# Modulation vectors as products of transposed weight rows on VectorE in a fused transformer kernel (one core, float32)

## The chip, the cores and the metric

The kernel runs as one program on one core of a Trainium2 chip. The metric is device time in microseconds for one execution. The kernel before takes 2101.35 us (median of 3 runs, 2100.73 to 2102.05).

## The reference

Two blocks of two layers each work on 256 tokens of width 1024; the first layer also carries 256 context tokens, so its units see 512 columns and all later ones 256. Everything is float32. What the change touches is the modulation: each of the four layers has a matrix of 1024 x 6144 that is multiplied with one or two vectors of 1024, and the result shifts, scales and gates the activations.

```python
silu_c, silu_cc = silu(c), silu(c_ctx)
for l in range(2):                                   # first block
    sh1, sc1, g1, sh2, sc2, g2 = split(silu_c @ w_mod[l] + b_mod[l], 6)
    csh1, ..., cg2 = split(silu_cc @ w_mod[l] + b_mod[l], 6)      # context, used in l = 0 (and sh1, sc1 of l = 1)
    m = mixer(x * (1 + sc1) + sh1)                   # Fourier, neighbourhood and latent attention, gates, w_out
    x = layer_norm(ALPHA * x + (1 + g1) * m)
    f = (silu(h @ w_gate) * (h @ w_up)) @ w_down     # h = x * (1 + sc2) + sh2, hidden width 2816
    x = layer_norm(ALPHA * x + (1 + g2) * f)
for i in range(2):                                   # second block: recurrent mixer, pool mixer, squared-relu MLP
    mod = silu(c_2) @ w_mod_2[i] + b_mod_2[i]
    ...
```

## The kernel before

The program is a list of units that every engine walks in the same order. A unit computes 512 output columns of one projection in four tiles m = 0 to 3, each with 8 tiles k of 128 rows. Weights are split in two float32r parts: ScalarE writes the high part SH (L509), VectorE the rest SL (L515), and TensorE makes three products for each (m, k), L556 to L558. The split for the next unit runs while this unit's products run; SH and SL have one buffer for each m. The raw weights come in two pairs RAW0, RAW1 of 1 MB by SyncE (L503), each issued when the split of the unit before has read that pair. Banks 0 to 3 of PSUM take the four tiles.

Beside the projections the 4 x 12 modulation chunks of 512 columns are computed. Four are made in the opening; the other 44 are hosted, one for each unit. There are two ways:
- `Side` (30 chunks). SyncE loads the chunk, 2 MB with 2 KB runs, into SIDE (L359). TensorE multiplies it with the columns CC of the vectors in 8 products of 512 columns (L373, 16 records in a trace), ahead of tile m = 3 (or of the unit's first product where the unit goes by k). VectorE transposes the result in blocks (L378), TensorE gathers it into columns at the unit's end (L326), VectorE adds the bias (L395).
- `SideOnDve` (14 chunks, two in single units and the twelve of the loop of the first layer's feed-forward). VectorE multiplies and adds the 8 row tiles, 512 elements each (L417 once, L421 seven times), transposes (L426), sums (L428); TensorE gathers (L437), VectorE adds the bias (L450).

The feed-forward of the first block has five single units and a loop of two turns over six units (four `UpGated`, two `Down`), for each layer. Between layers stands a norm that needs the last unit's complete result. SyncE, ScalarE and VectorE are in-order queues: what stands behind a wait is late with it.

Of the kernel before, what the change touches and what calls it, by code (L numbers as in the profile page):

```python
# [21 lines left out]
ALU = mybir.AluOpType  # L22
ACT = mybir.ActivationFunctionType
AX = mybir.AxisListType
# [100 lines left out]
class Counts:  # L125
# [30 lines left out]
    def up(self, name, by=1):  # L156
# [9 lines left out]
           "chunk2_loaded", "chunk3_loaded", "side_loaded", "out_done"],  # L166
# [3 lines left out]
            "tap_done", "tile_squared", "out_high", "gate_copied", "gate_open"],  # L170
    "dve": ["weight_low", "dve_read", "side_summed", "side_flipped", "side_added", "dve_done", "centred", "input_low", "one_minus_a2", "scanned",
# [9 lines left out]
def build(nc, A, out, const):  # L181
# [48 lines left out]
    U = MACC[:, 4:8, :].rearrange("p a b -> p (a b)").rearrange("p (t g n) -> p t g n", t=2, g=4)  # L230

# [38 lines left out]
    EARLY1, EARLY3 = (sb(f"EARLY{j}", [P, KT, 512], at=at) for j, at in ((1, AH_AT), (3, YH_AT)))  # L270
    EARLY2 = reg("EARLY2", 2048, [P, KT, 512])
# [43 lines left out]
    wmod = [A["w_mod"][0], A["w_mod"][1], A["w_mod_2"][0], A["w_mod_2"][1]]  # L315
    bmod = [("b_mod", 0), ("b_mod", 48), ("b_mod_2", 0), ("b_mod_2", 48)]
# [13 lines left out]
    class Side:  # L330
# [13 lines left out]
        def sp(self, e, K, j):  # L344
# [3 lines left out]
            if K.s("side_summed"):  # L348
                e.wait_ge(sem["side_summed"], K.at("side_summed"))
# [11 lines left out]
        def sums(self, e, K, m):  # L361
            pass
# [36 lines left out]
    class SideOnDve(Side):  # L399


        flip_at = 2

        def __init__(self, mat, chunk, per_turn=0, parts=((0, range(0, 3)), (1, range(3, KT)))):
            super().__init__(mat, chunk, per_turn)
            self.v = 0 if mat < 2 else 2
            self.parts = dict(parts)

        def pe_rows(self, e, K, j):
            pass  # L410

        def sums(self, e, K, m):
            for k in self.parts.get(m, ()):
                v = CC[:, k, self.v:self.v + 1]
                if k == 0:
                    e.wait_ge(sem["side_loaded"], K.at("side_loaded", 16))
                    e.tensor_scalar(MODROW[:, :], SIDE[:, k, :], v, None, ALU.mult).then_inc(K.up("dve_done"), 1)  # L417
                    continue
                e.wait_ge(sem["dve_done"], K.own("dve_done"))
                last = k == KT - 1  # L420
                e.scalar_tensor_tensor(out=MODROW[:, :], in0=SIDE[:, k, :], scalar=v, in1=MODROW[:, :], op0=ALU.mult,  # L421
                                       op1=ALU.add).then_inc(K.up("side_summed" if last else "dve_done"), 1)

        def flip(self, e, K, j):
            e.wait_ge(sem["side_summed"], K.own("side_summed"))
            e.transpose(VAR[:, :], MODROW[:, :]).then_inc(K.up("dve_done"), 1)  # L426
            e.wait_ge(sem["dve_done"], K.own("dve_done"))
            e.tensor_reduce(SIDESUM[:, :], VAR[:, :].rearrange("p (b i) -> p b i", i=32), AX.X, ALU.add) \  # L428
                .then_inc(K.up("side_flipped"), 1)

        def pe_turn(self, e, K, j):
            reader, count = K.bank[5]
            e.wait_ge(sem[reader], K.value(reader, count))
            e.wait_ge(sem["side_flipped"], K.at("side_flipped", j + 1))
            blocks = SIDESUM[:, :].rearrange("p (q a) -> p q a", a=4)
            for a in range(4):
                ins = e.matmul(PS[5][32 * a:32 * a + 32, 0:4], CON[:, C_SEL:C_SEL + 32], blocks[:, :, a],  # L437
                               start=True, stop=True)
            ins.then_inc(K.up("side_turned"), 1)
            K.bank[5] = ("side_added", K.s("side_added") + j + 1)  # L440

        def dve(self, e, K, j):
            e.wait_ge(sem["side_turned"], K.at("side_turned", j + 1))
            c = self.at(K)
            name, first = bmod[self.mat]
            t, r = place[name]
            dyn = K.turn is not None and self.per_turn
            dst = MODT[:, self.mat, bass.ds(4 * c, 4), self.v] if dyn else MODT[:, self.mat, 4 * c:4 * c + 4, self.v]
            bias = VEC[:, t, bass.ds(4 * c + (r + first), 4)] if dyn else VEC[:, t, r + first + 4 * c:r + first + 4 * c + 4]
            e.tensor_tensor(dst, PS[5][:, 0:4], bias, ALU.add).then_inc(K.up("side_added"), 1)  # L450


    class Unit:
# [129 lines left out]
        def act(self, e, K):  # L583
            for m in range(4):
                if self.mid and m == 2:
                    self.mid.act(e, K)
                e.wait_ge(sem["products"], K.at("products", self.freed(m)))
                self.read_act(e, K, m)
                if self.nxt:
                    self.nxt.split_act(e, K, m, 1 if self.loaded else 2)  # L590

# [585 lines left out]
    class LoadTransform(Load):  # L1177
        def act(self, e, K):

            e.wait_ge(sem["x_turned"], K.at("x_turned"))  # L1180
            if K.s("hidden_low"):
                e.wait_ge(sem["hidden_low"], K.at("hidden_low"))
# [1205 lines left out]
    def sides(layer):  # L2388

        return iter(SIDES[layer])  # L2390

# [266 lines left out]
```

## Time and profile before

| | |
|---|---|
| median of 3 runs | 2101.35 us |
| profiled execution, its own time | 2110.2 us |
| its span | 2108.4 us |
| TensorE busy | 1967.2 us (93%) |
| VectorE busy | 1266.3 us (60%) |
| ScalarE busy | 854.2 us (41%) |
| DMA moved | 332.09 MB, mean 158 GB/s |
| granted TensorE clock, mean | 0.966 |

Busy means that an instruction of the engine was under way; on TensorE the records overlap, so what a product costs is the distance from start to start.

### The profile page before, as it was taken

How to read it: one execution, taken by the hardware profiler on the slowest of the kernel's cores; microseconds unless marked ns; L12 is line 12 of the kernel's file. 1: busy time of each engine (PE TensorE's matmuls, PEld its weight loads, DVE VectorE, ACT ScalarE, POOL GpSimd, SP SyncE). 2: the span in 40 equal slices, each digit the busy share in tenths (PEclk: the TensorE clock that was granted, in tenths of full speed). 3: DMA queues.
4: the chain of work that ended last, by engine and by line, in shares of the span. 5: the costliest groups of instructions: out<-in, count | busy, mean ns of one | idle time of the engine just before them, and what ended most of it. 6: DMA issues, size and time to landing. Idle time of an engine off the chain costs nothing.

```text
span 2108.4 us, 32322 instructions
## 1 busy us (share of the span) xinstructions
PE 1967.2 (93%) x12568; PEld 1635.7 (78%) x12568; DVE 1266.3 (60%) x2212; ACT 854.2 (41%) x1382; POOL 129.9 (6%) x110
## 2 busy tenths in 40 slices
PE   5999999999999999998999888899998899988998
PEld 3786657467777788886886646789997789988998
DVE  5522453754666577678435474776667767776775
ACT  4322363264242222224335425344445744444444
POOL 0000000000300004012000000200111100000000
PEclk8999999999999999999999989999998999998999
DMA  9643403301545646555743331756564556653664
GB/s 331 189 140 106 154 11 127 88 11 42 188 141 168 230 160 220 178 193 166 217 162 101 111 104 61 251 189 201 180 218 140 163 177 202 198 160 100 195 190 136
DMA packets 280760, 332.09 MB, mean 158 GB/s; under 512 B 13190, under 2 KB 229692, under 8 KB 280508
## 3 DMA queue, kind: packets, MB, share of 16 engines
q1 hardware_dynamic: 268608, 323.05, 46.7%
q10 hardware_dynamic: 12028, 7.32, 1.4%
q8 instruction: 86, 1.41, 0.3%
q14 instruction: 38, 0.31, 0.0%
HBM read 329.31 MB, written 1.05 MB: 157 GB/s over the span
## 4 chain that ended last, share of the span: by engine, by line
PE 76%; DVE 10%; issue 6%; ACT 4%; DMA 3%; POOL 1%; ACTq 0%; DVEq 0%; POOLq 0%; SPq 0%
PE ps L556 19%; PE ps L557 18%; PE ps L558 18%; DVE SL L515 3%; PE ps L1427 2%; PE ps L373 2%; PE ps L1453 2%; ACT SH L509 2%; PE ps L1437 1%; PE ps L967 1%; PE ps L1702 1%; DMA RAW<-in_w_out 1%; PE ps L1342 1%; PE ps L1024 1%; PE ps L1706 1%
## 5 line engine op out<-in xcount | busy, mean ns | idle before, releaser
L515 DVE TENSOR_TENSOR SL<-RAW,SH 128x1024 fp32r<-128x1024 f32 (+2 forms) x448 | 524.7, 1173 | 447.9 <-ACT SH L509 443.4
L556 PE MATMUL ps<-AB,SH 128*128 128x256 f32 (+1 forms) x1856 | 602.3, 325 | 30.3 <-DVE AB L1104 19.4
L509 ACT ACTIVATE SH<-RAW 128x1024 fp32r<-128x1024 f32 (+2 forms) x448 | 444.1, 998 | 434.7 <-PE ps L558 270.2
L557 PE MATMUL ps<-AB,SH 128*128 128x256 f32 (+1 forms) x1856 | 594.9, 321 | 0.0
L558 PE MATMUL ps<-AB,SL 128*128 128x256 f32 (+1 forms) x1856 | 594.4, 320 | 0.0
L556 PEld LDWEIGHTS ps<-AB,SH 128*128 128x128 f32 x1856 | 355.5, 192 | 80.7 <-issue 32.5
L558 PEld LDWEIGHTS ps<-AB,SL 128*128 128x128 f32 x1856 | 353.8, 191 | 26.6
L557 PEld LDWEIGHTS ps<-AB,SH 128*128 128x128 f32 x1856 | 354.1, 191 | 25.2
L556 PE MATMUL ps<-HH,SH 128*128 128x256 f32 (+1 forms) x992 | 304.0, 306 | 6.6 <-DVE SL L515 2.6
L557 PE MATMUL ps<-HL,SH 128*128 128x256 f32 (+1 forms) x992 | 302.1, 305 | 0.0
L558 PE MATMUL ps<-HH,SL 128*128 128x256 f32 (+1 forms) x992 | 302.0, 304 | 0.0
L556 PEld LDWEIGHTS ps<-HH,SH 128*128 128x128 f32 x992 | 187.0, 188 | 21.8 <-issue 4.2
L558 PEld LDWEIGHTS ps<-HH,SL 128*128 128x128 f32 x992 | 186.2, 188 | 9.5
L557 PEld LDWEIGHTS ps<-HL,SH 128*128 128x128 f32 x992 | 186.2, 188 | 9.1
L813 POOL TENSOR_TENSOR S<-X 128x512 f32<-128x512 f32 (+1 forms) x6 | 11.6, 1930 | 1427.9 <-DVE X L840 1427.9
L556 PE MATMUL ps<-YB,SH 128*128 128x256 f32 (+1 forms) x256 | 84.7, 331 | 8.9 <-DVE YB L665 5.2
L557 PE MATMUL ps<-YB,SH 128*128 128x256 f32 (+1 forms) x256 | 83.1, 325 | 0.0
L558 PE MATMUL ps<-YB,SL 128*128 128x256 f32 (+1 forms) x256 | 83.1, 324 | 0.0
L819 POOL TENSOR_TENSOR S<-S,SQR 128x256 f32<-128x256 f32 (+1 forms) x51 | 54.0, 1059 | 450.9 <-ACT SQR L869 450.8
L421 DVE SCALAR_TENSOR_TENSOR MODROW<-SIDE,CC,MODROW 128x512 f32<-128x512 f32 x98 | 77.5, 791 | 3.0
L1502 ACT ACTIVATE PR<-ps,SM 128x512 f32<-128x512 f32 (+1 forms) x96 | 59.1, 616 | 38.4 <-PE ps L1437 28.9
L869 ACT ACTIVATE SQR<-X 128x256 f32<-128x256 f32 (+1 forms) x54 | 26.4, 488 | 118.4 <-PE ps L558 116.3
(295 smaller groups left out, 2418.1 us busy)
## 6 DMA issues: line engine op xcount, KB each, us to landing
SIDE<-in_w_mod SPq DMA_DIRECT2D x45, 2048.0 KB, 8.0
RAW<-in_ffn_w SPq DMA_DIRECT2D x64, 1024.0 KB, 5.4
RAW<-in_w_in SPq DMA_DIRECT2D x44, 1024.0 KB, 5.8
RAW<-in_w_ffn_gate SPq DMA_DIRECT2D x22, 1024.0 KB, 8.9
RAW<-in_w_ffn_up SPq DMA_DIRECT2D x22, 1024.0 KB, 5.4
RAW<-in_w_ffn_down SPq DMA_DIRECT2D x16, 1024.0 KB, 5.6
RAW<-in_w_branch SPq DMA_DIRECT2D x24, 512.0 KB, 3.5
RAW<-in_w_out SPq DMA_DIRECT2D x8, 1024.0 KB, 5.7
```

Of the source, the lines that this page charges most:

```text
L373: ins = e.matmul(PS[4][32 * g:32 * g + 32, :], CC[:, k, :], SIDE[:, k, :], start=k < 4, stop=k >= 4)
L421: e.scalar_tensor_tensor(out=MODROW[:, :], in0=SIDE[:, k, :], scalar=v, in1=MODROW[:, :], op0=ALU.mult, op1=ALU.add).then_inc(K.up("side_s ...
L509: e.activation(SH[:, m, 0:kt, :], RAW[p][:, 0:kt, o:o + P], ACT.Copy).then_inc(K.up("weight_high"), 1)
L515: e.tensor_tensor(SL[:, m, 0:kt, :], RAW[p][:, 0:kt, o:o + P], SH[:, m, 0:kt, :].bitcast(F32), ALU.subtract).then_inc(K.up("weight_low"), 1)
L556: e.matmul(ps, SH[:, m, k, :], xh, start=k == 0, stop=False)
L557: e.matmul(ps, SH[:, m, k, :], xl, start=False, stop=False)
L558: ins = e.matmul(ps, SL[:, m, k, :], xh, start=False, stop=k == self.kt - 1)
L819: e.tensor_tensor(S2[:, c0:c1], S2[:, c0:c1], SQR[:, t % 2, c0:c1], ALU.add).then_inc(K.up("square_added"), 1)
L869: e.activation(to, X[:, t, c0:c1], ACT.Square).then_inc(K.up("tile_squared"), 1)
L1427: e.matmul(self.scores_of(n), q, k, start=True, stop=True).then_inc(K.up("scores_done"), 1)
L1453: ins = e.matmul(o[64 * i:64 * i + 64, :], V[:, c0 // P + j, 64 * (h + i):64 * (h + i) + 64], PTS[pair % 2][:, i, j, :], start=j == 0, sto ...
L1502: e.activation(self.probs[:, n % self.depth, 0:c1 - c0], self.scores_of(n), ACT.Exp, bias=SM[:, n % 4:n % 4 + 1], scale=-1.0 if self.kind ...
```

## The change

Six of the 44 hosted chunks stay `Side`. The other 38 are computed by a new class `RowSums`. The host passes the modulation matrices transposed as further inputs, so that a row of 1024 holds the weights of one output column. SIDE is used as two slots; a load brings two such row tiles (1 MB, runs of 4 KB). ScalarE's queue loads the vectors, repeated over all 128 partitions, into VROW (a part of MACC) and applies silu there. For each row tile of 128 outputs and each vector VectorE multiplies the tile with the row of the vector and adds up along the free axis in one instruction (L463), and one addition per chunk puts in the bias (L485). No TensorE work is left in it. In the loop of the first layer every unit hosts two chunks (8 row tiles, four loads, of which SyncE issues two and ScalarE two), in the loop of the second layer half a chunk (2 row tiles, one load). Outside the loops the second layer's units and those of the second block host none. The six chunks (0,5) to (0,8), (0,10), (0,11) are computed for two vectors, all others for one.

```diff
-    class SideOnDve(Side):
+    class RowSums:
...
+            self.parts = parts or {1: {0: (0,), 2: (1,)}, 2: {-1: (0,), 0: (1,), 1: (2,), 2: (3,)},
+                                   4: {-1: (0, 1), 0: (2, 3), 1: (4, 5), 2: (6, 7)}}[self.halves]
+        def load(self, e, K, i, signal):
+            slot = self.slot(K, i)
+            if K.s("side_read") + i - 1 > 0:
+                e.wait_ge(sem["side_read"], K.at("side_read", i - 1))
...
+            e.dma_start(SIDE[:, 4 * slot:4 * slot + 4, :].rearrange("p (n a) b -> p n (a b)", n=2), src) \
+                .then_inc(K.up(f"{signal}{slot}_loaded", 16), 16)
+        def sp(self, e, K, j):
...
+            for i in range(min(2, self.halves)):
+                self.load(e, K, i, "half")
+        def act(self, e, K, m):
+            if m + 2 < self.halves:
+                self.load(e, K, m + 2, "later")
+        def sums(self, e, K, m):
+            for j in self.parts.get(m, ()):
...
+                for n, v in enumerate(vs):
+                    last = n == len(vs) - 1
...
+                    e.tensor_tensor_reduce(out=row if last else DUMP, in0=row, in1=VROW[v], op0=ALU.mult, op1=ALU.add, scale=1.0,
+                                           scalar=0.0, accum_out=SIDESUM[:, 8 * n + j:8 * n + j + 1]) \
+                        .then_inc(K.up("side_read" if last and a else "dve_done"), 1)
+        def dve(self, e, K, j):
+            e.wait_ge(sem["side_read"], K.own("side_read"))
...
+                e.tensor_tensor(dst, sums, bias.unsqueeze(2).to_broadcast([P, n, len(vs)]), ALU.add) \
+                    .then_inc(K.up("side_added"), 1)
...
+    SIDES = [
+        {"queries": Side(0, 4), "keys": RowSums(whole(0, 5, 0, 1)), "features": RowSums(whole(0, 6, 0, 1)),
+         "values": RowSums(whole(0, 7, 0, 1)), "gate 0 0": RowSums(whole(0, 8, 0, 1)), "gate 0 1": Side(0, 9),
+         "gate 1 1": Side(1, 0), "out 0": Side(1, 1), "out 1": Side(1, 2), "up 0": Side(1, 3),
+         "up 1": RowSums(whole(0, 10, 0, 1)), "up 2": RowSums(whole(0, 11, 0, 1)),
+         "down 0": RowSums(whole(3, 4, 2)), "down 1": RowSums(whole(3, 5, 2)),
+         "loop": [RowSums(whole(1, 4 + u, 0, per_turn=4) if u < 4 else whole(3, u - 4, 2, per_turn=2),
+                          whole(2, u, 2, per_turn=6)) for u in range(6)]},
+        {"loop": [RowSums((3, 24 + 2 * u, 2, 12, (2,))) for u in range(6)]},
+    ]
...
@@ -1268,6 +1335,8 @@
         def act(self, e, K):
+            if K.s("side_read"):
+                e.wait_ge(sem["side_read"], K.at("side_read"))
             for s in range(self.streams):
...
-                 ready=("input_low", True), by_k=half == 0, side=Side(2, 8 + half)) for half in range(2)]
+                 ready=("input_low", True), by_k=half == 0) for half in range(2)]
```

The wait in the diff's last part but one is in `Fourier`, whose buffer U shares MACC with VROW. In a unit's VectorE code `sums(m)` stands behind the split of tile m for the next unit, `sums(-1)` ahead of the unit's first wait; `act(m)` stands on ScalarE behind its split of tile m. New on ScalarE are also `LoadRows` (0.5 MB for each vector: two at the start, three ahead of the first layer's output projection, one in the second layer) and `SiluRows`.

TensorE in a unit of the first layer (the features), around the place of the hosted product; ps is a PSUM bank, AB the activations, CC the vectors:

```order
L558 MATMUL ps<-AB,SL 128x512
L373 MATMUL ps<-SIDE,CC 32x512 x8
L556 MATMUL ps<-AB,SH 128x512
L557 MATMUL ps<-AB,SH 128x512
L558 MATMUL ps<-AB,SL 128x512
```

The same place in the changed kernel (L593 to L595 are L556 to L558 of before); the gather of L326 at the unit's end is gone in the same way:

```order
L595 MATMUL ps<-AB,SL 128x512
L593 MATMUL ps<-AB,SH 128x512
L594 MATMUL ps<-AB,SH 128x512
L595 MATMUL ps<-AB,SL 128x512
```

Nothing but the projection's products is left on TensorE there.

VectorE in the first looped unit of the first layer before, from the split of tile 1 to the gated product of tile 2 (HT, HH, HL: hidden activations and their two parts):

```order
L515 TENSOR_TENSOR SL<-RAW_53,SH 128x1024
L419 REGISTER_ALU
L421 SCALAR_TENSOR_TENSOR MODROW<-SIDE,CC,MODROW 128x512
...
L426 STREAM_TRANSPOSE VAR<-MODROW 128x512
L427 REGISTER_ALU
L428 TENSOR_REDUCE SIDESUM<-VAR 128x16
L602 REGISTER_ALU
L895 ISA
L896 TENSOR_TENSOR HT<-ps,SG 128x512
```

and now (L463 stands twice for each row tile, the product and the reading of its sum; L552 is L515 of before, L935 is L896):

```order
L552 TENSOR_TENSOR SL<-RAW_53,SH 128x1024
L456 REGISTER_ALU
L463 ISA SIDE,SIDESUM<-SIDE,MACC 128x1024
L463 ISA SIDESUM 128x1
L463 ISA SIDE,SIDESUM<-SIDE,MACC 128x1024
L463 ISA SIDESUM 128x1
L641 REGISTER_ALU
L934 ISA
L935 TENSOR_TENSOR HT<-ps,SG 128x512
L936 ISA
L938 CAST HH<-HT 128x512
```

Before, the chunk's work ended ahead of tile 2; now a pair of row tiles stands behind each of the splits 0, 1 and 2, and a pair at the unit's head.

SyncE in the same loop now: a slot's two loads (L430) stand between the raw weights of one unit and those of the next, and the second waits until VectorE has read the last row tile of the unit before:

```order
L540 DMA RAW_54<-in_w_ffn_up 128x8x256
L427 REGISTER_ALU
L430 ISA
L430 DMA SIDE<-in_w_mod_t 128x2x1024
L427 REGISTER_ALU
L430 ISA
L430 DMA SIDE<-in_w_mod_t 128x2x1024
L539 REGISTER_ALU
L540 ISA
L540 DMA RAW_53<-in_w_ffn_gate 128x8x256
```

Before, one load (L359) stood there, which waited for L421.

## Rows read from the trace of the kernel before

**Rows 1.** The page: busy time by engine, and the chain that ended last.
```profile
PE 1967.2 (93%) x12568; PEld 1635.7 (78%) x12568; DVE 1266.3 (60%) x2212; ACT 854.2 (41%) x1382; POOL 129.9 (6%) x110
...
PE 76%; DVE 10%; issue 6%; ACT 4%; DMA 3%; POOL 1%; ACTq 0%; DVEq 0%; POOLq 0%; SPq 0%
```

**Rows 2.** Busy time by stretch: the two loops; columns PE, PEld, DVE, ACT, POOL, clock, DMA.
```profile
705.00:964.00 259.00, 259.00 (x1219) 211.50 (x1218) 187.28 (x258) 64.73 (x75) 35.59 (x20) 1.00 0.58 192
1425.00:1560.00 135.00, 135.00 (x1149) 135.00 (x1148) 86.43 (x117) 59.10 (x76) 15.47 (x17) 1.00 0.61 194
```

**Rows 3.** Timeline of PE around a hosted product: start, duration, instruction, [idle before].
```profile
1362.35 0.28 PE L557 MATMUL ps<-HL,SH 128*128 128x256 f32 x1
1362.47 0.28 PE L558 MATMUL ps<-HH,SL 128*128 128x256 f32 x1
1362.67 1.92 PE L373 MATMUL ps<-SIDE,CC 128*32 128x512 f32 x16
1364.53 0.38 PE L556 MATMUL ps<-HH,SH 128*128 128x256 f32 x1
1364.75 0.28 PE L557 MATMUL ps<-HL,SH 128*128 128x256 f32 x1
```

**Rows 4.** Timeline of PE around a gather at a unit's end.
```profile
644.88 0.39 PE L557 MATMUL ps<-AB,SH 128*128 128x512 f32 x1
645.11 0.39 PE L558 MATMUL ps<-AB,SL 128*128 128x512 f32 x1
645.43 0.25 PE L437 MATMUL ps<-SIDESUM,CON 128*32 128x4 f32 x8
645.60 0.50 PE L556 MATMUL ps<-AB,SH 128*128 128x512 f32 x1
645.94 0.39 PE L557 MATMUL ps<-AB,SH 128*128 128x512 f32 x1
```

**Rows 5.** Timeline of PE: hosted products and gathers beside waits.
```profile
1213.12 3.64 PE L373 MATMUL ps<-SIDE,CC 128*32 128x512 f32 x16 [4.13 <-DVE KR L1648]
...
1230.43 1.14 PE L1702 MATMUL ps<-CQ,SIDE 128*96 128x256 f32 x2 [3.87 <-DMA SIDE<-in_w_uv]
...
1354.12 0.25 PE L326 MATMUL ps<-MODROW,CON 128*32 128x12 f32 x8 [1.06 <-DVE MODROW L378]
...
1374.86 2.43 PE L373 MATMUL ps<-SIDE,CC 128*32 128x512 f32 x16
1377.22 0.39 PE L556 MATMUL ps<-AB,SH 128*128 128x256 f32 x1
...
1625.74 0.30 PE L326 MATMUL ps<-MODROW,CON 128*32 128x12 f32 x8 [6.27 <-DVE MODROW L378]
```

**Rows 6.** Timeline of VectorE in one looped unit of the first layer.
```profile
718.33 1.22 DVE L515 TENSOR_TENSOR SL<-RAW,SH 128x1024 fp32r<-128x1024 f32 x1 [0.55 <-ACT SH L509]
719.47 3.89 DVE L421 SCALAR_TENSOR_TENSOR MODROW<-SIDE,CC,MODROW 128x512 f32<-128x512 f32 x5
723.39 0.71 DVE L426 STREAM_TRANSPOSE VAR<-MODROW 128x512 f32<-128x512 f32 x1
...
724.75 0.68 DVE L896 TENSOR_TENSOR HT<-ps,SG 128x512 f32<-128x512 f32 x1
```

**Rows 7.** Timeline of VectorE: an instruction of the new kind on 512 elements.
```profile
252.93 0.73 DVE L1555 CUSTOM_DVE_ANT_1 ps<-ps,BIASZ 128x512 f32<-128x512 f32 x1
253.58 0.14 DVE L1555 DVE_READ_ACCUMULATOR2_ANT SM<- 128x1 f32 x1
```

**Rows 8.** DMA issues: count, size, median us from issue to landing.
```profile
SIDE<-in_w_mod SPq DMA_DIRECT2D x45, 2048.0 KB, 8.0
...
RAW<-in_w_ffn_up SPq DMA_DIRECT2D x22, 1024.0 KB, 5.4
```

**Rows 9.** Two stretches of 2 us, columns as in rows 2 (last GB/s).
```profile
706.00:708.00 2.00, 2.00 (x10) 1.64 (x9) 1.56 (x3) 0.44 (x1) 0.00 (x0) 1.00 1.07 407
710.00:712.00 2.00, 2.00 (x11) 1.65 (x10) 0.00 (x0) 0.60 (x1) 0.00 (x0) 1.00 1.10 348
```

More of the change, by code:

```diff
@@ L361, in sums @@
         def sums(self, e, K, m):
+            pass
+        def act(self, e, K, m):
             pass
@@ L396, in dve @@
                 .then_inc(K.up("side_added"), 1)
-    class SideOnDve(Side):
+    class RowSums:
         flip_at = 2
[L404 to L409, printed above, removed]
-            pass
[L412 to L440, printed above, removed]
-        def dve(self, e, K, j):
[L443 to L450, printed above, removed]
@@ new lines, in build, with __init__, slot @@
+        behind_gate = False
+        def __init__(self, *spans, parts=None):
+            self.spans = spans
+            self.pieces = [(mat, first + j, per_turn, vs) for mat, first, n, per_turn, vs in spans for j in range(n)]
+            self.halves = len(self.pieces) // 2
+            self.parts = parts or {1: {0: (0,), 2: (1,)}, 2: {-1: (0,), 0: (1,), 1: (2,), 2: (3,)},
+                                   4: {-1: (0, 1), 0: (2, 3), 1: (4, 5), 2: (6, 7)}}[self.halves]
+        def slot(self, K, i):
+            return (K.start["side_read"] + i) % 2
@@ new lines, in sums @@
+        def sums(self, e, K, m):
+            for j in self.parts.get(m, ()):
+                i, a = j // 2, j % 2
+                slot = self.slot(K, i)
+                if a == 0:
+                    if i == 0:
+                        e.wait_ge(sem["rows_ready"], K.at("rows_ready"))
+                        e.wait_ge(sem["side_added"], K.own("side_added"))
+                    signal = f"{'half' if i < 2 else 'later'}{slot}_loaded"
+                    e.wait_ge(sem[signal], K.at(signal, 16))
+                vs = self.pieces[j][3]
+                row = SIDE[:, 4 * slot + 2 * a:4 * slot + 2 * a + 2, :].rearrange("p a b -> p (a b)")
+                for n, v in enumerate(vs):
+                    last = n == len(vs) - 1
+                    if not last and j:
+                        e.wait_ge(sem["dve_done"], self.dumped)
+                    e.tensor_tensor_reduce(out=row if last else DUMP, in0=row, in1=VROW[v], op0=ALU.mult, op1=ALU.add, scale=1.0,
+                                           scalar=0.0, accum_out=SIDESUM[:, 8 * n + j:8 * n + j + 1]) \
+                        .then_inc(K.up("side_read" if last and a else "dve_done"), 1)
+                    if not last:
+                        self.dumped = K.own("dve_done")
@@ L2409, in build @@
         tok = (0, N)
[L2410 removed]
+        side = SIDES[l].get
         if l == 0:
@@ L2466, in build @@
                         prep=prep_ln("ln1_g", "ln1_b", 8 * l, ALPHA, l, 3, streams)))
-        assert next(it, None) is None, "a modulation chunk has no place"
         def down(krow, kt, half, per, side, last):
```

117 lines of the change are left out of this document (80 added, 37 removed).

## The prediction

> **What bounds the kernel now.** I read the page's busy times first, then the chain that ended last: TensorE is busy 93% of the span and carries 76% of the chain, VectorE 10%, ScalarE 4%, DMA 3% [rows 1]. In both feed-forward loops TensorE never stops: 259 us of 259 and 135 of 135 [rows 2], VectorE at 72% and 64%. So what leaves TensorE there comes off the time, and what is added to VectorE is free as long as each split for the next unit is ready. The timelines then give the prices. The sum is made against the profiled execution's 2110.2 us (span 2108.4, 1.8 lie around it). The median of the runs is 2101.35, 8.9 below; I take the difference over unchanged. From run to run 0.2% (4 us) is what a measurement can tell from no change.
>
> **Taken off TensorE.** A hosted product stands between two projection products whose starts are 0.12 us apart in steady work (1362.35, 1362.47). From 1362.47 to the next projection product at 1364.53 are 2.06, less 0.12 is 1.94, and the following start is 0.22 later instead of 0.12: 2.04 us [rows 3]. A gather, in a unit of 512 columns: 645.11 to 645.60 is 0.49 against 0.23, and 645.94 comes 0.34 later instead of 0.23: 0.37 us [rows 4]. Of the 30 `Side` 24 go, with product and gather, and 14 gathers of `SideOnDve`. Not all are worth their price:
> - Three products stand ahead of a by-k unit whose first projection product waits for the norm anyway (queries and first up unit of layer 2, first convolution). At 1374.86 the product and its gap fill the time until 1377.22 [rows 5]: 0. A fourth, in the second convolution, is followed by a wait of 6.27 us for VectorE [rows 5], which is the bound there: 0 as well, and VectorE gets back one transpose, 0.7.
> - The other 20 stand in running work: 20 x 2.04 = 40.8.
> - Of 38 gathers I drop 7 beside norms, Fourier parts and the convolutions: 31 x 0.37 = 11.5.
> - Two gathers of the second layer wait for the transpose on VectorE: 1.06 at 1354.12 [rows 5] and about as much in another up unit. What is queued behind is ready. 2.
> - The hosted product of gate 1 1 in layer 2 waits 4.13 us for a bank that the latent norm on VectorE frees, and the units behind start late; ScalarE then issues the latent weights only after this unit, and TensorE waits 3.87 us for them at 1230.43 [rows 5]. With the product gone tile 3 runs at once and the weights go out earlier. Of 8.0 I take 6; below it 0, above it 11 if the half-clock stretch behind these stops goes as well.
>
> Together 0.7 + 40.8 + 11.5 + 2 + 6 = 61.
>
> **Added to VectorE, and its cover.** No row shows the new instruction with 1024 elements from SBUF. The nearest is one of its kind with 512, a PSUM and an SBUF operand: from 252.93 to 253.58 it takes 0.65 us, and the reading of its sum hides in the next one [rows 7]. A split reads two long SBUF operands, 1024 elements in 1.22 us, and the gated product 512 in 0.68 [rows 6]: 512 elements more cost 0.54, so I take 0.65 + 0.54 = 1.19. From below 1.14 (a split to its successor, 718.33 to 719.47). From above 1.56, two of the L421 with 512 elements (3.89 / 5 each) [rows 6], and farther off 2.4 if two SBUF operands took two passes. I go by the instruction of the same kind.
>
> In a looped unit of layer 1 (96 products at 0.227 us and a gather: 22.16) VectorE is busy 187.28 / 259 x 22.16 = 16.0 us [rows 2]. Out go one L417 (about 0.5), seven L421 (5.4) and from 723.39 to 724.75 the transpose and the sum (1.4), 7.3 in all [rows 6]. In come 8 x 1.19 and two small additions, 9.8. That is 18.5 of the 21.8 us that TensorE then needs, so TensorE still hides it. In layer 2's loop (135 us for 12 units, 11.25 each) 86.43 / 135 x 11.25 = 7.2 [rows 2] become 7.2 + 2 x 1.19 + 0.15 = 9.7: hidden too, with little over. If the cover goes, lateness comes slowly. The split of tile m is made a quarter of a unit into the current one and used only when the next unit reaches tile m, so it may be three quarters late, less the 2 to 3 us that it takes: 14 us in layer 1, 6 in layer 2.
>
> **Loads.** A looped unit of layer 1 now moves 6 MB instead of 4. 1 MB (1.05e6 bytes) takes 3.0 us in runs of 1 KB (348 GB/s) and 2.6 in runs of 2 KB (407) [rows 9]; I take 2.6 for the new runs of 4 KB. 2 x 3.0 + 4 x 2.6 = 16.4 of 21.8 us, so the sum fits. What counts is the round of dependences, because SyncE issues the next unit's raw weights only behind the load that waits for the last L463 of the unit before. Once round in layer 1: the half chunk and the raw pair land (2.6 + 3.0 + 2.4, the last being what 5.4 us for 1 MB leave over 3.0 [rows 8]), ScalarE splits (1.05), it issues the next half, which lands (2.6 + 2.4, up to 8 where it shares the engines), then on VectorE two row tiles 2.4, the gated product with its two parts 1.8, the split 1.1 and two row tiles 2.4. That is 21.8 to 24.8 us against 21.8. VectorE can fall behind by 0 to 3 us a unit over 12 units. Slack swallows 14 of it inside the loop, but what is open at the loop's end lies on the path, since the norm waits for the last X. In layer 2 the round is: the raw pair behind a load (or two) 8.0 (5.4 to 11.0), split on ScalarE 1.05 and on VectorE 1.15, row tile 1.2, split 1.15, together 12.5 (9.9 to 15.5) against 11.25. Only part of the units meets the worst phase. I take 1 us for layer 1 and 4 for layer 2, the latter mostly at the loop's end; the ends are 0 and 35 together.
>
> The Trainium skill ("DMA: Bandwidth & Descriptors", the section on where 436 GB/s comes from) says that for loads from HBM a core's share of about 358 GB/s binds. The row has 407 GB/s, so here the measurement decides. By 358 a new load would take 2.9 us, the round of layer 1 up to 0.9 more.
>
> **Other waits.** In the first layer Fourier's copies on ScalarE now wait until gate 0 0's last row tile is read. The unit `values` holds its splits back to its end, so its own six L463 behind them (7.1 us) push gate 0 0's eight (9.5) and four half splits (2.8) back, with one load between (about 6 us landing, 4 of it a wait): counted from the end of `values` they end at 25, and TensorE wants the first copy about 24.4 after the same point (22.2 for the unit, 2.2 for the gather and the first Fourier products). So 1 us, from 0 to 7 if the clock falls behind the stop. The 3 MB of vectors beside other loads and ScalarE's silus, where that engine is half idle: 1, from 0 to 4.
>
> **Sum.** -61 + 1 + 4 + 1 + 1 = -54. The profiled 2110.2 becomes 2056, the median 2101.35 - 54 = 2047 us.
>
> **Rivals.**
> - The loops give part of it back. For it speak VectorE at 85% of a unit in both loops, loads at 75%, and rounds whose upper ends lie above the unit's time. Against it the slack of 14 and 6 us. A middle case: 24 us a unit in layer 1 is 12 x 2.2 = 26 late, 12 us in layer 2 is 12 x 0.75 = 9; both come due by the loop's end. 35 instead of 5: +30, less a third that the first units still hide, gives 2047 + 20 = 2067.
> - In the second layer and block splits and raw weights set the pace, and the freed time turns into waits for them. For: the layer has a clock below 1 and several short waits. Then its 12 products in running work, its gathers and the waits behind them, 24.5 + 4 + 2 + 6 = 37, give only 6: 2047 + 31 = 2078. Against: its loop, with units as long as those before it, has TensorE busy 135 of 135 us [rows 2].
> - Slower: the new instruction takes two passes, 2.4 us. A looped unit of layer 1 then needs 16.0 - 7.3 + 8 x 2.4 + 0.3 = 28.2 us of VectorE against 21.8: 12 x 6.4 = 77. Layer 2's loop 12.1 against 11.25: 11. Fourier 10. 2101 - 60 + 98 = 2139. It decides from 1.6 us an instruction on, where VectorE fills a unit of layer 1, and the kernel is slower than before from about 2.05. For: L421 takes 0.78 for 512. Against: 0.65 for the same kind [rows 7], and the splits, which read two SBUF operands in one pass [rows 6].
> - The change doesn't act: products of the first layer leave, but a unit stays 22.2 and 24.3 us long since its loads set it. Loads are 16.4 of 21.8, so I give it next to nothing; the time would be about 2101 - 10 = 2091.
>
> **How the numbers follow.** Forecast 0.70, its own range 2034 to 2062. Loops 0.15, second layer 0.09, two passes 0.04, no action 0.02. The range 2033 to 2074 takes in the loops' case and leaves out about 0.17. Faster by over 0.2%: all but the slow case and a little of the last, 0.94. Within 0.2%: 0.02. Slower: 0.04.
>
> **What would show it.** Right: in the profile after, L373's successor (L381) has 96 records, not 480; the loops' units are 21.8 and 11.2 us apart and TensorE stays at 259 of 259; L463 is about 1.2 us from start to start; TensorE at the latent projection of layer 2 waits under 3 us. Wrong: waits of TensorE for SL of L552 in the loops, ScalarE waiting for L463 at its own loads, VectorE waiting for SIDE, a stop at Fourier, or L463 over 1.6 us.

## The result, and the profile after

The changed kernel ran in 2084.04 us (median of 14 runs, 2070.3 to 2097.0), the kernel before beside it on the same chip in 2106.51 (14 runs): ratio 0.9897, 95% interval 0.9870 to 0.9924. That is 1.0% or 22 us faster (16 to 27), where 54 were forecast. On the 2101.35 us of the prediction the ratio makes 2080 us, outside its range.

The page of the profiled execution after (2083.5 us, span 2081.6, granted clock 0.957 on average against 0.966 before): TensorE's busy time, the chain's shares by engine and by line, the groups of the new row product L463 and of GpSimd's L858, and two DMA issues. They answer to [rows 1, 8].

```profile
PE 1914.5 (92%) x11880; PEld 1631.6 (78%) x11880; DVE 1368.9 (66%) x2406; ACT 858.4 (41%) x1389; POOL 150.5 (7%) x110
...
PE 63%; DVE 16%; DMA 8%; issue 7%; ACT 5%; POOL 1%; SPq 0%; ACTq 0%; DVEq 0%; POOLq 0%
PE ps L593 15%; PE ps L595 15%; PE ps L594 15%; DVE SL L552 4%; DVE SIDE L463 4%; ACT SH L546 2%; DMA RAW<-in_w_ffn_down 2%; PE ps L1496 2%; PE ps L1522 2%; PE ps L1006 2%; PE ps L1506 1%; DMA RAW<-in_w_ffn_gate 1%; DMA RAW<-in_w_out 1%; PE ps L1771 1%; DMA RAW<-in_w_in 1%
...
L463 DVE CUSTOM_DVE_ANT_0 SIDE<-SIDE,MACC 128x1024 f32<-128x1024 f32 x152 | 208.9, 1398 | 1.6 <-DMA SIDE<-in_w_mod_t 1.2
...
L858 POOL TENSOR_TENSOR S<-S,SQR 128x256 f32<-128x256 f32 (+1 forms) x51 | 70.7, 1386 | 425.7 <-ACT SQR L908 425.7
...
SIDE<-in_w_mod_t SPq DMA_DIRECT2D x52, 1024.0 KB, 5.0
...
RAW<-in_w_ffn_down SPq DMA_DIRECT2D x16, 1024.0 KB, 7.3
```

Of before, for the last of these:

```profile
RAW<-in_w_ffn_down SPq DMA_DIRECT2D x16, 1024.0 KB, 5.6
```

TensorE has 53 us of busy time less than before, 1914.5 against 1967.2, so the products and gathers did leave it. But the span is only 26.8 shorter, and TensorE's share of the chain fell from 76 to 63% while VectorE's rose from 10 to 16 and DMA's from 3 to 8. The other half of what left TensorE is not saved: part of it is now spent in waits. L463 has a mean of 1398 ns, and the raw down weights take 7.3 us to land instead of 5.6.

The two loops, busy time by engine (PE, PEld, DVE, ACT, POOL, clock, DMA), up to the first product of the norm behind each, answer to [rows 2]:

```profile
705.00:968.00 263.00, 247.72 (x1079) 203.87 (x1077) 222.05 (x328) 62.10 (x74) 49.87 (x24) 0.97 0.79 269
1397.00:1547.00 150.00, 138.89 (x1185) 137.75 (x1183) 120.85 (x182) 63.74 (x84) 34.10 (x24) 0.97 0.78 266
```

Before, TensorE was busy 259 of 259 and 135 of 135 us. Now it stands still for 15 and 11 us. Most of the 15 and half of the 11 are the wait of the norm behind the loop, which [rows 2] leave out. All traces hold the same 9792 products of split weights with activations (the three of L593 to L595 and their like), so the n-th can be set beside the n-th. These starts are read from the traces, the last column from the changed kernel's second one; negative is ahead of before:

```
product of 9792                       before us   after   run again
384   first branch, first layer          198.0     -7.3     -8.7
1248  first out unit                     536.4    -13.5    -14.7
1440  first behind the norm              601.2    -11.6     -7.4
1872  feed-forward loop, layer 1         705.5    -17.4    -13.1
2832  last two down units of that loop   927.1    -20.2    -15.5
3024  first behind the norm              985.8     -2.6     +2.3
4896  feed-forward loop, layer 2        1433.9    -33.4    -29.1
6048  first behind the norm             1591.4    -23.3    -21.3
6912  second block                      1733.0    -33.3    -31.3
9791  last                              2099.5    -26.7    -33.6
```

Three stretches give time back: the out units (1.9 us from 1248 to 1440, in the second trace 7.3), the end of layer 1's loop (17.6) and layer 2's loop (10). A single pair of traces tells such a stretch to some 5 us (last section). The stops of TensorE there (start, duration, instruction, [idle before <-releaser]):

```profile
167.56 0.80 PE L1328 MATMUL ps<-MACC 128*128 128x256 f32 x1 [2.80 <-ACT MACC L1347]
...
550.82 0.25 PE L331 MATMUL ps<-MODROW,CON 128*32 128x12 f32 x8 [3.16 <-DVE MODROW L386]
...
919.08 0.79 PE L593 MATMUL ps<-HH,SH 128*128 128x512 f32 x1 [3.23 <-DVE HL L940]
...
968.24 0.58 PE L1006 MATMUL ps<-ONES,S 128*128 128x1 f32 x2 [11.40 <-POOL S L858]
...
1453.15 0.39 PE L593 MATMUL ps<-HH,SH 128*128 128x256 f32 x1 [2.57 <-DVE HL L940]
...
1547.45 0.80 PE L1006 MATMUL ps<-ONES,S 128*128 128x1 f32 x3 [5.62 <-POOL S L858]
```

The 11.4 us at 968.24 are the largest: the norm waits for GpSimd's last sum. Before it was 2.04:

```profile
973.48 0.72 PE L967 MATMUL ps<-ONES,S 128*128 128x1 f32 x5 [2.04 <-POOL S L819]
```

The new instruction itself, L463: min, median and max of its durations in ns.

```profile
L463 DVE CUSTOM_DVE_ANT_0 SIDE<-SIDE,MACC x152: 1212/1221/2327, 81.7 to 1543.3; 128x1024 f32<-128x1024 f32 x152
L463 DVE CUSTOM_DVE_ANT_0 EARLY<-SIDE,MACC x24: 1216/1218/1226, 80.6 to 653.0; 128x1024 f32<-128x1024 f32 x24
```

The median is what was forecast (start to start it is 1.14 us), but the maximum is 2327. Of the 176 row products 28 took 1.7 to 2.33 us, 22 of them in the looped down units of layer 1, 6 in those of layer 2, none anywhere else. VectorE and then GpSimd in one such stretch:

```profile
791.73 1.22 DVE L552 TENSOR_TENSOR SL<-RAW,SH 128x1024 fp32r<-128x1024 f32 x1
792.86 2.32 DVE L463 CUSTOM_DVE_ANT_0 SIDE<-SIDE,MACC 128x1024 f32<-128x1024 f32 x1
795.12 2.30 DVE L463 CUSTOM_DVE_ANT_0 SIDE<-SIDE,MACC 128x1024 f32<-128x1024 f32 x1
...
798.13 1.21 DVE L552 TENSOR_TENSOR SL<-RAW,SH 128x1024 fp32r<-128x1024 f32 x1
```

```profile
791.89 2.21 POOL L852 TENSOR_TENSOR S<-X 128x512 f32<-128x512 f32 x1 [214.71 <-DVE X L879]
794.06 2.27 POOL L858 TENSOR_TENSOR S<-S,SQR 128x512 f32<-128x512 f32 x1
798.37 2.12 POOL L852 TENSOR_TENSOR S<-S,X 128x512 f32<-128x512 f32 x1 [2.04 <-DVE X L879]
```

They take turns. GpSimd's sum L852 starts at 791.89 beside the split and ends at 794.10, though such a sum takes 1.29 us where VectorE leaves it alone. The row product that starts at 792.86 ends 1.1 us after that, at 795.18. L858, started at 794.06, ends at 796.33, 1.15 after the row product, and the next row product ends at 797.42, 1.1 after that. All 28 slow row products overlap a sum of GpSimd, and none of the other 148 does.

ScalarE in the loop of layer 1 (what it waited for: us in total, times, longest):

```profile
ACT SH L546 <- DMA RAW<-in_w_ffn_gate: 48.3, 6, 12.3
ACT SH L546 <- DMA RAW<-in_w_ffn_down: 39.9, 4, 14.3
```

### The profile page after: what moved, and what is told of

The parts are those of the page before. It is cut to its first block, busy times and chain, and to the rows that moved or that the text cites. A ratio compares the mean times of both kernels' runs of the same rounds, so it can differ in the third digit from the quotient of the medians.

```text
span 2081.6 us, 31284 instructions
## 1 busy us (share of the span) xinstructions
PE 1914.5 (92%) x11880; PEld 1631.6 (78%) x11880; DVE 1368.9 (66%) x2406; ACT 858.4 (41%) x1389; POOL 150.5 (7%) x110
## 4 chain that ended last, share of the span: by engine, by line
PE 63%; DVE 16%; DMA 8%; issue 7%; ACT 5%; POOL 1%; SPq 0%; ACTq 0%; DVEq 0%; POOLq 0%
PE ps L593 15%; PE ps L595 15%; PE ps L594 15%; DVE SL L552 4%; DVE SIDE L463 4%; ACT SH L546 2%; DMA RAW<-in_w_ffn_down 2%; PE ps L1496 2%; PE ps L1522 2%; PE ps L1006 2%; PE ps L1506 1%; DMA RAW<-in_w_ffn_gate 1%; DMA RAW<-in_w_out 1%; PE ps L1771 1%; DMA RAW<-in_w_in 1%
## 5 line engine op out<-in xcount | busy, mean ns | idle before, releaser
L552 DVE TENSOR_TENSOR SL<-RAW,SH 128x1024 fp32r<-128x1024 f32 (+2 forms) x448 | 520.1, 1163 | 398.6 <-ACT SH L546 395.8
L593 PE MATMUL ps<-AB,SH 128*128 128x256 f32 (+1 forms) x1856 | 600.5, 324 | 34.8 <-DVE AB L1143 22.7
L595 PE MATMUL ps<-AB,SL 128*128 128x256 f32 (+1 forms) x1856 | 595.5, 321 | 0.0
L593 PEld LDWEIGHTS ps<-AB,SH 128*128 128x128 f32 x1856 | 356.4, 192 | 73.1 <-issue 32.8
L595 PEld LDWEIGHTS ps<-AB,SL 128*128 128x128 f32 x1856 | 356.6, 192 | 26.3
L593 PE MATMUL ps<-HH,SH 128*128 128x256 f32 (+1 forms) x992 | 306.3, 309 | 14.3 <-DVE HL L940 8.3
L595 PE MATMUL ps<-HH,SL 128*128 128x256 f32 (+1 forms) x992 | 304.5, 307 | 0.0
L463 DVE CUSTOM_DVE_ANT_0 SIDE<-SIDE,MACC 128x1024 f32<-128x1024 f32 x152 | 208.9, 1398 | 1.6 <-DMA SIDE<-in_w_mod_t 1.2
L593 PEld LDWEIGHTS ps<-HH,SH 128*128 128x128 f32 x992 | 188.3, 190 | 27.3 <-DVE HL L940 9.1
L595 PEld LDWEIGHTS ps<-HH,SL 128*128 128x128 f32 x992 | 189.4, 191 | 9.7
L852 POOL TENSOR_TENSOR S<-X 128x512 f32<-128x512 f32 (+1 forms) x6 | 11.5, 1924 | 1386.8 <-DVE X L879 1386.8
L858 POOL TENSOR_TENSOR S<-S,SQR 128x256 f32<-128x256 f32 (+1 forms) x51 | 70.7, 1386 | 425.7 <-ACT SQR L908 425.7
L593 PE MATMUL ps<-YB,SH 128*128 128x256 f32 (+1 forms) x256 | 83.9, 328 | 11.3 <-DVE YB L704 4.8
L595 PE MATMUL ps<-YB,SL 128*128 128x256 f32 (+1 forms) x256 | 83.2, 325 | 0.0
```

The costliest lines, as they stand in the source:

```text
L463: e.tensor_tensor_reduce(out=row if last else DUMP, in0=row, in1=VROW[v], op0=ALU.mult, op1=ALU.add, scale=1.0, scalar=0.0, accum_out=SIDE ...
L552: e.tensor_tensor(SL[:, m, 0:kt, :], RAW[p][:, 0:kt, o:o + P], SH[:, m, 0:kt, :].bitcast(F32), ALU.subtract).then_inc(K.up("weight_low"), 1)
L593: e.matmul(ps, SH[:, m, k, :], xh, start=k == 0, stop=False)
L595: ins = e.matmul(ps, SL[:, m, k, :], xh, start=False, stop=k == self.kt - 1)
L858: e.tensor_tensor(S2[:, c0:c1], S2[:, c0:c1], SQR[:, t % 2, c0:c1], ALU.add).then_inc(K.up("square_added"), 1)
```

## The experiments

Each was timed in five rounds against the kernel before; the changed kernel ran once more beside small sums, PSUM rows and ScalarE's load, and the others are compared with it through their ratios to the kernel before. Ratios below are to that kernel, with the 95% interval in brackets. A gain over the changed kernel is the difference of two ratios times 2105 us, and is good to some 8 us. Theories: P, VectorE and GpSimd hold each other up while both read SBUF; R, the round of dependences of the prediction (raw weights stand on SyncE behind a load that waits for the last L463); L, VectorE is simply full.

**The changed kernel again.**

> The changed kernel once more, as the yardstick for the runs beside it. 0.990 of the kernel before; in its layer-1 loop 28 of the 96 row products (L463) take about 2.2 us and not 1.22, all of them beside an addition on GpSimd.

0.9892 (0.9865 to 0.9919), the same as the first time. Its trace has 27 slow row products where the first has 28. The 28 of the expectation were those of both loops: 22 of 96 in layer 1's and 6 of 24 in layer 2's.

**Small sums on GpSimd.**

```diff
         c0, c1 = tokens
+        if K.turn is not None:
+            c1 = c0 + 16
         def total(t):
```

> Left out: most of GpSimd's running sums for the norm in the looped down units (16 columns of 512 or 256 are added). Theory P (VectorE and GpSimd hold each other up while both read SBUF): no L463 of the loops is over 1.3 us, TensorE's 11.4 us wait at the norm behind the layer-1 loop shrinks to 2 to 4, that loop gets 10 to 15 us shorter and the kernel 10 to 18 us: ratio to before 0.982 to 0.985. Theory R (the raw weights stand behind a load that waits for the last L463, whatever GpSimd does): under 4 us gained, 0.988 to 0.990. Theory L (VectorE is simply full at 8 row products a unit): L463 may be shorter, but the waits stay; under 4 us.

0.9770 (0.9739 to 0.9801), 26 us better than the changed kernel and more than expected. In the looped down units the sums run over 16 columns only, the rest is left out. All 176 row products take 1.2 us. TensorE at the norm behind layer 1's loop:

```profile
955.64 0.61 PE L1008 MATMUL ps<-ONES,S 128*128 128x1 f32 x4 [1.19 <-POOL S L860]
```

From product 2832 to 3024 this trace loses nothing (-16.3 to -18.3 against before). So in layer 1's loop the row products were not too many for VectorE; L falls there, and R by itself falls too.

**The same sums left out of the kernel before, as a control.**

> The kernel before, with most of GpSimd's running sums for the norm in the looped down units left out (16 columns are added). A control for the port theory: if GpSimd's additions cost only where row products stand beside them, the kernel before gains 0 to 4 us here (the waits of 2.04 and 1.46 us at the two norms behind the loops get a little shorter), ratio 0.998 to 1.000. If it gains 10 us and more too, the small sums themselves were worth that, and the run with small sums in the changed kernel says nothing on the row products.

0.9987 (0.9965 to 1.0009). The small sums alone are worth 3 us (0 to 7), so some 23 of the 26 us, and 13 at the least with the intervals of all three ratios, lie in what they did to the changed kernel's own work.

**The row of the vector from PSUM.** Nothing is left out here. The rows lie in banks 4 to 7, which the loops leave free.

```diff
+    PROW = {0: BANKS[:, 2048:3072], 2: BANKS[:, 3072:4096]}
...
+                        e.activation(PROW[v], VROW[v], ACT.Copy)   # once per layer
...
-  in0=row, in1=VROW[v], ...
+  in0=row, in1=PROW[v] if self.psum else VROW[v], ...   # loops, down 0, down 1
```

> In the loops (and the two down units ahead of them) L463 takes its second factor, the row of the vector, from a PSUM copy and not from SBUF, so it reads SBUF once. The work is the same, and two or three copies of 1 us come in on ScalarE. Theory P: L463 stays at 1.2 to 1.3 us beside GpSimd's additions, and these take 1.3 and not 2.2; gain as with the small sums, 10 to 18 us, ratio 0.982 to 0.985. Theories R and L: nothing, 0.989 to 0.991. If a PSUM operand over two banks is slower (1.4 us and more), the loop gets longer instead and says so in the length of L463 away from GpSimd.

0.9782 (0.9757 to 0.9807), 23 us better than the changed kernel and again more than expected. L463 is L466 in this kernel: its durations with the PSUM operand, two of them in a looped down unit, then GpSimd's sums over the same stretch and TensorE at the norm.

```profile
L466 DVE CUSTOM_DVE_ANT_0 SIDE<-SIDE,ps x128: 1207/1216/1223, 664.9 to 1532.7; 128x1024 f32<-128x1024 f32 x128
...
798.88 1.21 DVE L466 CUSTOM_DVE_ANT_0 SIDE<-SIDE,ps 128x1024 f32<-128x1024 f32 x1
800.02 1.21 DVE L466 CUSTOM_DVE_ANT_0 SIDE<-SIDE,ps 128x1024 f32<-128x1024 f32 x1
```

```profile
797.91 2.21 POOL L860 TENSOR_TENSOR S<-X 128x512 f32<-128x512 f32 x1 [216.71 <-DVE X L887]
800.08 1.29 POOL L866 TENSOR_TENSOR S<-S,SQR 128x512 f32<-128x512 f32 x1
```

```profile
957.58 0.58 PE L1014 MATMUL ps<-ONES,S 128*128 128x1 f32 x2 [2.21 <-POOL S L866]
```

1223 ns is now the maximum of 128. At 800.08 GpSimd's sum runs beside a row product in 1.29 us; at 797.91 one beside a split, which still reads SBUF twice, takes 2.21. The norm waits 2.21 us and not 11.4. This is P shown without leaving work out: the same products, in the same units, with one operand elsewhere. GpSimd's full sums are still there, and up to the norm's first products behind the loop the trace loses 2.3 us (product 2832 to 3024, -15.4 to -13.1) where the changed kernel's lost 17.6. The page "SBUF — State Buffer" of the Trainium skill, section "Who interferes with whom", has the rule: a VectorE instruction with two SBUF inputs contends with a GpSimd instruction that reads SBUF, and the later one is held until the earlier has finished; with at most one SBUF input, outside VectorE's two-port modes, they don't contend. The traces agree with both halves: 2.33 us against 1.22.

**The second half chunk's load from ScalarE.**

```diff
-            for i in range(min(2, self.halves)):
+            for i in range(1 if self.halves == 4 else min(2, self.halves)):
                 self.load(e, K, i, "half")
         def act(self, e, K, m):
+            if m == -1:            # at the start of the unit
+                if self.halves == 4:
+                    self.load(e, K, 1, "mid")
+                return
```

> In the layer-1 loop the second of the four half-chunk loads is issued by ScalarE at the start of the unit, so the raw weights of the next unit no longer stand behind it on SyncE. Theory R: ScalarE's waits for raw gate and down weights (88 us in 10 waits) fall to under 30, the norm's wait goes from 11.4 to under 4 us, 8 to 14 us gained (0.983 to 0.986). Theory P: the waits of ScalarE get shorter but VectorE is late all the same; 0 to 4 us (0.988 to 0.990).

0.9836 (0.9813 to 0.9858), 12 us better: more than P alone had allowed for, about what R had. ScalarE's waits for raw gate and down weights in the loop fall from 88 us to 4. But 30 row products are still slow, and the norm's wait is 8.12 us, not the under 4 of R:

```profile
962.70 0.59 PE L1012 MATMUL ps<-ONES,S 128*128 128x1 f32 x2 [8.12 <-POOL S L864]
```

The two looped down units, 790 to 835 us in this kernel, and below them about the same units with PSUM rows (busy PE, PEld, DVE, ACT, POOL):

```profile
790.00:835.00 45.00, 45.00 (x201) 37.24 (x200) 44.65 (x56) 12.87 (x16) 26.33 (x12) 1.00 0.70 236
```

```profile
792.00:835.00 43.00, 43.00 (x191) 35.62 (x190) 33.30 (x58) 12.76 (x17) 20.32 (x12) 1.00 0.86 296
```

With the raw weights in time VectorE is busy 44.65 of 45 us: it is the bound of the down units, by the row products' waits for GpSimd. With PSUM rows it is busy 33.30 of 43. So R was real, but as the second link: it stretches a lateness that P makes. With small sums or PSUM rows and R left as it was, ScalarE still waits 58 and 41 us for these weights, and TensorE hardly loses anything by it.

**The vectors' loads behind the out units.**

```diff
-        seq.append(LoadRows(*((0, 1, 2) if l == 0 else (2,))))
         for half in range(2):
             seq.append(Residual(...))
+        seq.append(LoadRows(*((0, 1, 2) if l == 0 else (2,))))
         seq.append(Norm(...))
```

> The changed kernel with the loads of the vectors (L1238, 1.5 MB in layer 1, 0.5 in layer 2) behind the second out unit, ahead of the norm, and not ahead of the first out unit. Theory V (they delay the raw weights of out 1, whose first split comes 4.4 us late against the shift of 13.5): ScalarE's wait for in_w_out falls from 19.4 to about 15 us, the transpose of the hosted product is on time, TensorE's stop of 3.2 to 4.1 us at 551 goes, and 3 to 6 us are gained (ratio 0.986 to 0.988). Rival: they only move and delay the splits of the first up units as much; 0 (0.989 to 0.990).

0.9867 (0.9834 to 0.9900): 5 to 6 us better by the ratios, which the interval doesn't resolve from the changed kernel. The traces do. ScalarE in the changed kernel, the load of the first vector and its first split for out 1, and below that split in this kernel:

```profile
530.22 0.33 ACTq L1238 DMA_DIRECT2D MACC<-in_c  x1
543.62 1.06 ACT L546 ACTIVATE SH<-RAW 128x1024 fp32r<-128x1024 f32 x1 [19.41 <-DMA RAW<-in_w_out]
```

```profile
537.00 1.06 ACT L546 ACTIVATE SH<-RAW 128x1024 fp32r<-128x1024 f32 x1 [15.65 <-DMA RAW<-in_w_out]
```

The split comes 6.6 us earlier, 3.7 of it against the units around it, since this trace was 2.9 us ahead. The stop of 3.16 us at 550.82 is gone, and from product 1248 to 1440 the kernel loses nothing (-16.4 to -18.1, against -13.5 to -11.6 and -14.7 to -7.4 of the changed one). The other traces bear it out: the four further kernels with the later loads have no such stop and lose at most 0.6 us there, the four further kernels with the early loads have it (3.6 to 5.0 us) and lose 6.6 to 7.8.

**The combinations.** PSUM rows, ScalarE's load and later vectors together; then the same without ScalarE's load; then without the PSUM rows.

> Three edits together: the vector rows from PSUM in the loops, the second half chunk's load from ScalarE, and the vectors' loads behind the out units. If they are independent: 20 us (PSUM rows) + 3 to 6 (later loads) + up to 3 (what ScalarE's issue still gives once VectorE is on time) ahead of the changed kernel, ratio to before 0.975 to 0.978. If the PSUM rows already give all that the loop had to give, ScalarE's issue adds nothing: 0.976 to 0.978. If the gain of ScalarE's issue (11 us by itself) adds to it in full: 0.972.

> The vector rows from PSUM and the vectors' loads behind the out units, the second half chunk's load on SyncE again. If ScalarE's issue still gives something once VectorE is on time: 0.977 to 0.978, that is 0.002 to 0.003 above the three edits together (0.975). If the round of dependences costs nothing then: as the three edits, 0.974 to 0.975.

> The changed kernel with the second half chunk's load on ScalarE and the vectors' loads behind the out units, the rows still from SBUF. By themselves these gave 0.9836 and 0.9867 against 0.9892 and 0.9897 of the changed kernel. Independent: 0.981. The rest to the three edits (0.975), 12 us, is then what reading both factors from SBUF costs when the splits are on time; the wait at the norm behind layer 1's loop stays at about 8 us here, since GpSimd's additions still hold the row products to 2.2 us.

0.9747 (0.9718 to 0.9775), 0.9745 (0.9712 to 0.9779) and 0.9822 (0.9791 to 0.9853). With the row products at 1.2 us ScalarE's load adds nothing that can be told: the round costs only what P has made late. In the second of them the loop of layer 1 loses nothing (product 2832 to 3024: -22.1 to -22.5), and the norm's first product has about the wait that it had before, 2.22 us against 2.04:

```profile
950.86 1.95 PE L1014 MATMUL ps<-ONES,S 128*128 128x1 f32 x16 [2.22 <-POOL S L866]
```

Both are 53 us under the kernel before, about the forecast 54, once the slow row products and the vectors' loads are mended, though layer 2's loop still loses more than was forecast. Their profiled executions had mean granted clocks of 0.958 and 0.964, that of the changed kernel 0.957: the clock is not what separates them from it. Of the third there is only the trace of an execution of 10355 us, five times its other six, which can't be used; its time is 16 us above the first, which is what the PSUM rows still give beside the two other edits.

**Layer 2's loop.** First the changed kernel with small loads; then, on the three edits, small row products; then, on the three edits, another place for one row product. The first two leave work out: 960 of 1024 columns of each load, 1008 of 1024 elements of each product. Theories for the loads and for the row products are R2 and V2.

```diff
+            if self.halves == 1:
+                src, dst = src[:, :, 0:64], dst[:, :, 0:64]      # small loads
...
+                if self.halves == 1:
+                    row = row[:, 0:16]                           # small row products
...
+ RowSums(..., psum=True, parts={0: (0,), 1: (1,)})               # other place
```

> The changed kernel; in layer 2's loop each half chunk's load brings 64 of 1024 columns only, so the sums there are of old data; the row products (L463) read as much as ever. Theory R2 (the raw weights stand behind a load in the queue and land late): ScalarE's waits for raw weights in the loop drop from about 75 us to under 40, both stops of 2.5 us at the third and ninth boundary and most of the 5.6 us at the norm go, 6 to 10 us gained (0.984 to 0.987). Theory V2 (VectorE has too much to do in these units): 0 to 2 us (0.989).

> The three edits together, and in layer 2's loop the row products multiply 16 of 1024 elements (so that those sums are left out), their loads as before. What VectorE's share of the loss there is: if the row products (24 x 1.1 us) make it, both boundary stops shrink from 2.5 to 3 us to under 1.5 and the wait at the norm from 3.5 to about 2, in all 4 to 6 us: 0.972 to 0.973. If it is the loads and the landing of raw weights: under 2 us, 0.974 to 0.975.

> The three edits of before together, and in layer 2's loop the second row product of a unit stands behind tile 1 and not behind tile 2, so that the late split of tile 2 no longer has it between itself and the gated product on which the first down unit waits. Theory: each of the two stops of 2.5 to 3 us at the boundary from the last up to the first down unit loses the 1.14 us of the row product, 2 us together: 0.001 under the three edits (0.9737). Rival: the row product waits for its load at tile 1 and the split of tile 2 gets later instead: 0 to 0.002 worse.

Small loads: 0.9880 (0.9850 to 0.9911), not told apart from the changed kernel; from product 4896 to 6048 its trace loses 7.1 us against 10.1 and 7.8 in the two of the changed kernel. The stops that R2 said would go are still there, 2.07 and 2.39 us at the boundaries and 4.93 at the norm, so the loads don't make them. Small row products: 0.9677 (0.9647 to 0.9706), 15 us under the three edits and more than either theory gave. In its trace the loop gains 5.2 us where the kernel with the three edits loses 5.4, both boundary stops are gone, and the norm's wait is the 1.46 us of before, where the three edits have 4.11 and the changed kernel has 5.62:

```profile
1514.46 0.72 PE L1022 MATMUL ps<-ONES,S 128*128 128x1 f32 x5 [1.46 <-POOL S L874]
```

So in layer 2 the row products are the load: 2.3 us in a unit of 11.25 stand between late splits and the gated products. The other place: 0.9729 (0.9694 to 0.9764), by the median the fastest kernel here that leaves nothing out, but not told apart from 0.9745. One of the two boundary stops of 2.5 us goes and the other shrinks to 1.85, but the norm's wait grows to 5.25.

## Why the prediction was wrong

The step that failed is the price of a row product on VectorE, 1.19 us wherever it stands, and with it that TensorE hides VectorE's work in the loops. In the looped down units of layer 1 a row product takes 2.3 us beside a sum of GpSimd, and no term of the sum had GpSimd in it. Term by term:

- **Off TensorE, -61: right, as far as the traces can tell.** In the kernel with PSUM rows and later vectors the shift is -11 at product 576, -22 at the last units of layer 1's loop and -56 ahead of layer 2's. (That kernel has the loads elsewhere, but the same work off TensorE.) The kernel before itself differs by 1 to 9 us between its trace and that of the control from product 1248 on, so this is no closer check than that. L381 has the 96 records that were named, and the waits of TensorE at the latent projection (4.13 and 3.87 us before) have become 1.95, under the 3 that was named.
- **Added to VectorE: this step failed.** The price of 1.19 us was good for 148 of 176 row products. The other 28 took 27 us more, and 24 of these 27 us fell into the four looped down units of layer 1, 6 a unit. There VectorE needs 22.3 us against TensorE's 21.8; with PSUM rows it needs 16.7. The prediction had the number, 2.4 us, but as a rival in which every instruction takes two passes, and that was excluded by rows that stood away from GpSimd. It never asked what else reads SBUF in the unit. The trace of before held the answer twice. Of its 380 splits of 1024 elements 32 took 1.33 to 1.79 us instead of 1.22, and each of the 32 starts while a GpSimd instruction is under way. And the very instruction whose 0.78 us the prediction quoted shows it too. L421, its durations and four of them in a down unit, and GpSimd beside it:

```profile
L421 DVE SCALAR_TENSOR_TENSOR MODROW<-SIDE,CC,MODROW x98: 743/752/1776, 633.0 to 961.6; 128x512 f32<-128x512 f32 x98
...
825.30 5.05 DVE L421 SCALAR_TENSOR_TENSOR MODROW<-SIDE,CC,MODROW 128x512 f32<-128x512 f32 x4
```

```profile
824.26 2.27 POOL L813 TENSOR_TENSOR S<-S,X 128x512 f32<-128x512 f32 x1
828.33 1.47 POOL L819 TENSOR_TENSOR S<-S,SQR 128x512 f32<-128x512 f32 x1 [1.81 <-ACT SQR L869]
```

Four of 752 ns would take 3.0 us, but these take 5.05: two of them met a sum. Of the 98 in all, 94 take 0.75 us, and the 4 that start while a sum is under way take 1.66 to 1.78. (Where a sum starts while an L421 is under way, it is the sum that takes longer.)

- **Layer 1's loop, +1: it was +18.** P made the down units late, R carried it to the raw weights (ScalarE's waits of up to 14.3 us above), and, as the prediction said of whatever is open at the loop's end, it fell on the norm. The 0 to 35 given as the ends of both loops together hold it; the value taken was wrong, since it came from a round with row products at 1.2 us. With them at 1.2 us the end of the loop loses at most 0.5 us in the traces of small sums and of the kernels with PSUM rows and later vectors (2.3 with PSUM rows alone), as forecast.
- **Layer 2's loop, +4: about +10 to 15.** The pair of traces loses 10 there, but before ran this loop at the slower of the two paces of the last section; against the control's trace, which ran it at the faster, it is 15. The small row products give 10 us in the traces for what the loop still loses with the three edits, 15 in the times. The 6 slow row products there are some 3 us of it. The round as forecast counted one of the two row products. The first down unit needs the hidden values at once, and these stand behind a split and a row product: that was not counted. How much each of the two makes was not measured.
- **Vectors, +1: about +5.** The load was priced by ScalarE's half idle time; it was the raw weights of out 1 beside it that came 4 us late.
- **Fourier, +1: 2.** The stop grew from 0.69 to 2.80 us.
- **The rivals.** By its number the nearest to 2080 is the second, 2078 with 0.09: in the second layer and block the freed time turns into waits. That is luck. From product 3024 to 4896 the changed kernel gains 31 us on before, so that stretch gave the time after all; it was lost in the loops. By its mechanism the nearest is "the loops give part of it back", 2067 with 0.15. It took late rounds in all twelve units, though; here the lateness began in the down units, with the slow row products.

Together: -61 + 18 + 10 + 5 + 2 = -26, against the 26.7 of the two traces. That this comes out so near is partly luck. The 5 are from other traces than the rest (this pair lost 1.9 there), and the pair also lost 6.6 us behind product 6912, where it was the changed kernel that ran at the slower pace and the second trace gained 2.3.

## What to carry to other kernels

Before a VectorE instruction with two SBUF operands is put into a stage, look in that stage for GpSimd instructions that read SBUF: each overlap costs up to the whole of the other's time, here 1.1 us on 1.2. Moving one operand to PSUM took it away here, and cost nothing in the instruction's duration (1216 ns against 1221); look for free banks. A single mean duration hides this; read min, median and max of the nearest group, and ask why its maximum is more than twice its median.

## What was not expected of the hardware

The pace of TensorE's products differs between executions at the same granted clock. The changed kernel in two stretches, and in its second trace in the later one (x is the count of matmuls in 50 us, clock 1.00 in all):

```profile
1750.00:1800.00 50.00, 50.00 (x443) 50.00 (x443) 36.39 (x55) 22.29 (x27) 0.00 (x0) 1.00 0.63 195
1960.00:2010.00 50.00, 50.00 (x426) 50.00 (x426) 34.51 (x53) 20.92 (x27) 0.00 (x0) 1.00 0.58 183
```

```profile
1960.00:2010.00 50.00, 50.00 (x444) 50.00 (x443) 35.70 (x54) 22.05 (x27) 0.00 (x0) 1.00 0.62 193
```

426 against 444 in the same work, 4% less, with no wait in between. From start to start the products are 113.3 ns apart on average at one pace and 117.8 at the other. One trace keeps one pace over hundreds of us and then changes. The kernel before ran layer 2's loop at the slow pace and the changed one at the fast, some 5 us in favour of the change; at the end it was the other way round. The control, which is the kernel before but for its small sums, ran that loop at the fast pace and gained 5.1 us on it there. The times of one kernel spread over 1% in these runs. What sets the pace stays open.
